# A prompt's attention between the key units of a sampling kernel: issued in smaller pieces over 21 units, with another order of value buffers

## The reference, cut to what matters

```python
o_dn = rms_norm(o_dn) * norm_w * jax.nn.silu(dn_z)          # delta rule's output
...
o_mb = moba_attend(mq, k_all, v_all, pos0)                  # blocks of 256 keys, best 3 and the own one
y = jnp.concatenate([o_dn, o_mb], axis=-1) @ w_out
...
logits = (jnp.einsum('bhqd,bhqrsd->bhqrs', qi, kg) * scale - slopes[:, None, None, None] * dist)
p = jax.nn.softmax(jnp.where(allowed, logits, NEG_INF).reshape(bsz, h, qc, r * MOBA_BLOCK), axis=-1)
out = jnp.einsum('bhqrs,bhqrsd->bhqd', p, vg)
```

## Time and profile before

| | |
|---|---|
| median of 3 runs | 1178.69 us (1176.52 to 1180.17) |
| the profiled execution | 1179.3 us |
| its span, first to last instruction | 1177.6 us |
| mean granted TensorE clock | 0.956 of 2.4 GHz |
| PE, DVE, ACT, POOL busy | 93%, 60%, 46%, 26% of the span |

### The profile page before, as it was taken

How to read it: one execution, slowest core, us unless ns; L and a number is a source line. 1 busy time by engine, 2 the same in 40 slices (tenths; PEclk the granted TensorE clock), 3 DMA queues, 4 the chain that set the end, 5 groups by cost and what they waited for, 6 DMA issues and landing times.

```text
span 1177.6 us, 20042 instructions
## 1 busy us (share of the span) xinstructions
PE 1091.5 (93%) x6991; PEld 984.7 (84%) x6991; DVE 704.3 (60%) x1200; ACT 543.8 (46%) x858; POOL 300.6 (26%) x285
## 2 busy tenths in 40 slices
PE   6999979877999999897999999989999799999997
PEld 5999869655666666486999999979999799999996
DVE  4843643666777777648666663365564866665344
ACT  3337511254766666435444443343333544444324
POOL 8400123310767677334000000223003400000111
PEclk9989969987999999798999999989999899999998
DMA  7334200356989897542444443434445244444321
GB/s 230 131 124 149 72 1 1 97 202 211 320 298 304 295 317 246 188 147 71 155 142 142 142 143 126 150 128 143 143 143 153 72 142 142 148 157 159 128 94 45
DMA packets 120882, 182.59 MB, mean 155 GB/s; under 512 B 6224, under 2 KB 61615, under 8 KB 120750
## 3 DMA queue, kind: packets, MB, share of 16 engines
q1 hardware_dynamic: 118402, 174.61, 44.7%
q0 software_dynamic: 2416, 7.16, 2.1%
HBM read 176.12 MB, written 5.63 MB: 154 GB/s over the span
## 4 chain that ended last, share of the span: by engine, by line
PE 80%; DVE 11%; issue 3%; ACT 3%; DMA 1%; POOL 0%; SPq 0%; DVEq 0%; ACTq 0%; POOLq 0%
PE bank L1724 74%; PE bank L2035 4%; DVE kTl L1147 2%; DVE lo L1140 1%; DMA raw<-w_in_mix 1%; DVE xres L1571 1%; ACT hi L748 1%; DVE xres L1147 1%; PE bank L2235 0%; PE bank L2166 0%; DVE sbias L1445 0%; DVE gs L1441 0%; DVE sbias L1436 0%; DVE xl L1578 0%; ACT kTh L748 0%
## 5 line engine op out<-in xcount | busy, mean ns | idle before, releaser
L1724 PE MATMUL bank<-xh,hi 128*128 128x320 f32 x1184 | 373.2, 315 | 27.1 <-DVE xl L1578 18.3
L1724 PE MATMUL bank<-xl,hi 128*128 128x320 f32 x1184 | 370.2, 313 | 0.0
L1724 PE MATMUL bank<-xh,lo 128*128 128x320 f32 x1184 | 369.7, 312 | 0.0
L1140 DVE TENSOR_TENSOR lo<-raw,hi 128x2048 fp32r<-128x2048 f32 x102 | 241.4, 2366 | 188.5 <-ACT hi L748 188.5
L748 ACT ACTIVATE hi<-raw 128x2048 fp32r (+2 forms) x112 | 205.3, 1833 | 113.6 <-PE bank L1724 110.7
L1724 PEld LDWEIGHTS bank<-xh,hi 128*128 128x128 f32 x1184 | 226.3, 191 | 31.1 <-issue 25.8
L1724 PEld LDWEIGHTS bank<-xl,hi 128*128 128x128 f32 x1184 | 226.6, 191 | 0.1
L1724 PEld LDWEIGHTS bank<-xh,lo 128*128 128x128 f32 x1184 | 226.2, 191 | 0.0
L1724 PE MATMUL bank<-hh,hi 128*128 128x320 f32 x416 | 129.5, 311 | 1.3 <-DVE hraw L1147 1.3
L1724 PE MATMUL bank<-hh,lo 128*128 128x320 f32 x416 | 128.6, 309 | 0.0
L1724 PE MATMUL bank<-hl,hi 128*128 128x320 f32 x416 | 128.5, 309 | 0.0
(11 more groups left out here) (397 smaller groups left out, 1554.6 us busy)
## 6 DMA issues: line engine op xcount, KB each, us to landing
raw<-w_up SPq DMA_DIRECT2D x44, 1024.0 KB
kring<-cache_k SPq DMA_DIRECT2D x88, 256.0 KB, 3.7
vring<-cache_v SPq DMA_DIRECT2D x88, 256.0 KB, 4.8
raw<-w_down SPq DMA_DIRECT2D x8, 2048.0 KB
raw<-w_in_mix SPq DMA_DIRECT2D x6, 2048.0 KB
raw<-cache_k SPq DMA_DIRECT2D x40, 256.0 KB, 3.6
raw<-cache_v SPq DMA_DIRECT2D x40, 256.0 KB, 5.1
raw<-w_in_sc SPq DMA_DIRECT2D x8, 1024.0 KB
```

The lines of the kernel that those rows point to most:

```text
L1140: dve.tensor_tensor(lo[:, p], weight(n)[:, :, 256 * p:256 * p + 256], hi[:, p], ALU.subtract)\
L1724: return pe.matmul(out, lhsT, rhs, start=start, stop=stop, **kw)
```

## The change

The prompt's work is laid over units 0 to 20 instead of 0 to 15; the last five are units 0 to 4 of round 1. Exponential, normalisation, gate product and halves of the delta rule's output are done in two pieces of two heads each (two instructions where there was one). The maxima, exponentials and divisions of the two query tiles stand at separate units, as do the copies of V's rows. TensorE's stages move from units 0, 1, 4, 6, 11, 13 to 0, 2, 7, 10, 15, 19, and the third group of the turn becomes a stage of its own at 17. That group goes into bank 5, after ACT has copied the first group from it (new wait on pTsb0), no longer into bank 7. `own_scores(0)` waits for kvtok5, since it uses bank 7. `pT` moves by 512 columns, to the ring's last two value pairs. The value pages' order becomes: the two pairs in `raw` first, then the ring's four. SP's wait for po1 moves from key group 6 to group 8, and a wait for pT2 comes in at group 7. The output weights' second half waits for all but two value pairs, before for all but four. The table of exponentials on ACT is loaded at unit 1 instead of 0. The numbers of the key units' own steps do not change.

```diff
-        pT = vr[:, 1536:3072]
-        PROMPT = {0: "sums", 1: "kv0", 4: "scores", 6: "kv1", 11: "turn", 13: "values"}
+        pT = vr[:, 2048:3584]
+        PROMPT = {0: "sums", 2: "kv0", 7: "scores", 10: "kv1", 15: "turn", 17: "turn1", 19: "values"}
...
-        vpages = [vring[:, i] for i in range(4)] + [spare_raw[:, 4:6], spare_raw[:, 6:8]]
+        vpages = [spare_raw[:, 4:6], spare_raw[:, 6:8]] + [vring[:, i] for i in range(4)]
...
-                if n == V_LAG // 2:
+                if n == V_LAG // 2 + 1:
+                    PE.wait(sp_, "pT2")
+                if n == V_LAG // 2 + 2:
                     PE.wait(sp_, "po1")
...
-            sp_.wait_ge(s["v_lo"], VALL - 4)
+            sp_.wait_ge(s["v_lo"], VALL - 2)
...
             def prompt(u):
-                if u == 0:
-                    o_logs((2, 3))
+                if u in (0, 1):
+                    o_logs((2 + u,))
+                if u == 1:
                     act.preload_act_table(ACT.Exp)
+                if u in (2, 3):
+                    x = slice(2 * u - 4, 2 * u - 2)
                     AC.wait(act, "oln3")
-                    AC.up(act.activation(qg[:, :, :], qg[:, :, :], ACT.Exp, scale=-0.5), "orn")
-                if u == 3:
-                    DV.wait(act, "mixo")
-                    AC.up(copy(xh[:, 0:4, :], oT), "mixh_done")
+                    AC.up(act.activation(qg[:, x, :], qg[:, x, :], ACT.Exp, scale=-0.5), f"orn{u - 2}")
+                if u == 5:
                     act.wait_ge(s["stores"], 16 * 7)
-                    kv_rows(range(3))
-                if u == 7:
-                    kv_rows(range(3, 6))
-                if u in (8, 9):
-                    for h in range(H):
-                        t, i = u - 8, 4 * (u - 8) + h
+                    DV.wait(act, "on11")
+                    kv_rows((0, 1))
+                if u in (6, 7):
+                    x = slice(2 * u - 12, 2 * u - 10)
+                    DV.wait(act, f"mixo{u - 6}")
+                    AC.up(copy(xh[:, x, :], oT[:, x, :]), f"mixh{u - 6}")
+                if u == 6:
+                    kv_rows((2,))
+                if 9 <= u <= 12:
+                    for i in (2 * u - 18, 2 * u - 17):
+                        t, h = divmod(i, H)
                         DV.wait(act, f"pmax{t}")
                         x = pl0[:, h, :] if t == 0 else pl1[:, h, :]
                         AC.up(act.activation(x, x, ACT.Exp, bias=pst[:, 0, i:i + 1], accum_out=pst[:, 1, i:i + 1]),
                               f"pexp{i}")
-                if u == 12:
-                    for g in range(3):
+                if 11 <= u <= 13:
+                    kv_rows((u - 8,))
+                if u in (16, 18):
+                    for g in ((0, 1) if u == 16 else (2,)):
                         PE.wait(act, f"pT{g}")
-                        AC.up(copy(pT[:, 512 * g:512 * g + 512], bank[5 + g][:, :]), f"pTsb{g}")
-                if u == 15:
+                        AC.up(copy(pT[:, 512 * g:512 * g + 512], bank[(5, 6, 5)[g]][:, :]), f"pTsb{g}")
+                if u == 20:
                     for t in range(2):
...
-                    if b == 0:
-                        prompt(u)
+                    prompt(b * UNITS + u)
...
-                if u == 1:
-                    AC.wait(dve, "orn")
-                    DV.up(tt(oT, oT, qg[:, :, :], ALU.mult), "on1")
-                if u == 2:
-                    DV.wait(dve, "on1")
-                    DV.up(dve.scalar_tensor_tensor(out=oT, in0=oT, scalar=vec(0, PA_NW), in1=zsb[:, :, :], op0=ALU.mult,
-                                                   op1=ALU.mult), "mixo")
-                if u == 4:
-                    AC.wait(dve, "mixh_done")
-                    DV.up(tt(xl[:, 0:4, :], oT, xh[:, 0:4, :], ALU.subtract), "mixl_done")
-                if u == 5:
+                if u in (3, 4):
+                    x = slice(2 * u - 6, 2 * u - 4)
+                    AC.wait(dve, f"orn{u - 3}")
+                    DV.up(tt(oT[:, x, :], oT[:, x, :], qg[:, x, :], ALU.mult), f"on1{u - 3}")
+                if u in (5, 6):
+                    x = slice(2 * u - 10, 2 * u - 8)
+                    DV.wait(dve, f"on1{u - 5}")
+                    DV.up(dve.scalar_tensor_tensor(out=oT[:, x, :], in0=oT[:, x, :], scalar=vec(0, PA_NW), in1=zsb[:, x, :],
+                                                   op0=ALU.mult, op1=ALU.mult), f"mixo{u - 5}")
+                if u in (7, 8):
+                    x = slice(2 * u - 14, 2 * u - 12)
+                    AC.wait(dve, f"mixh{u - 7}")
+                    DV.up(tt(xl[:, x, :], oT[:, x, :], xh[:, x, :], ALU.subtract), f"mixl{u - 7}")
+                if u == 8:
...
-                if u == 6:
+                if u == 9:
...
-                if u in (5, 6):
-                    t, x = u - 5, (pl0, pl1)[u - 5]
+                if u in (8, 10):
+                    t, x = (u - 8) // 2, (pl0, pl1)[(u - 8) // 2]
...
-                if u in (10, 11):
-                    t, x = u - 10, (pl0, pl1)[u - 10]
+                if u in (11, 13):
+                    t, x = (u - 11) // 2, (pl0, pl1)[(u - 11) // 2]
...
-                if u == 15:
+                if u == 20:
...
-                if stage == "turn":
+                if stage in ("turn", "turn1"):
                     AC.wait(pe, "kvtok5")
                     for g, (x, c0, t) in enumerate(((pl0, 0, 0), (pl1, 0, 1), (pl1, P, 1))):
+                        if (g < 2) != (stage == "turn"):
+                            continue
                         DV.wait(pe, f"pnorm{t}")
+                        if g == 2:
+                            AC.wait(pe, "pTsb0")
                         for h in range(H):
-                            ins = pe.transpose(bank[5 + g][:, P * h:P * h + P], x[:, h, c0:c0 + P], ident[:, :])
+                            ins = pe.transpose(bank[(5, 6, 5)[g]][:, P * h:P * h + P], x[:, h, c0:c0 + P], ident[:, :])
                         PE.up(ins, f"pT{g}")
...
-                    if b == 0 and u in PROMPT:
-                        prompt(PROMPT[u])
+                    if n in PROMPT:
+                        prompt(PROMPT[n])
...
+                        if b == 0:
+                            AC.wait(pe, "kvtok5")
```

## The result

The changed kernel took 1166.97 us (median of four runs, 1164.68 to 1173.07) against 1178.84 us before (four runs, 1176.52 to 1180.17): a ratio of 0.991 with an interval of 0.9895 to 0.9927, that is 8.6 to 12.4 us less. In a second set of five runs it was 1166.23 us and 0.990 (0.9881 to 0.9919). The forecast was 1171.2 us, 7.5 us less, with a range of 1167.5 to 1178.0.

A forecast was written before the change was run, and what follows sets the result against it. TensorE bounds the kernel, with 14.6 us idle plus low clock before turn(0). The walk's 10.5 us, less 2.5 clock and 0.5 hand-offs, gave 7.5; 1179.3 - 7.5 - 0.6 = 1171.2 us, range 1167.5 to 1178.0.

The forecast's parts named there:

- The walk: New lists stepped from the first key transpose (235.94): turn(0), the first probabilities' turn, at 285.3, 10.5 us earlier.
- One sign was missed: Sign named for the forecast: TensorE idle time before turn(0) below 8 us.
- Two were passed: Signs named for the forecast: turn(0) near 288 and the value stage near 278.
- The table load: ACT's table load, one unit later: 1.28 us, with the skill's 1.38 us drain left out.
- The middle: Prompt's scores to its turn: 13.0 us of DVE work in 15.1 us; new kvtok5 and pTsb0 waits taken as nothing.
- The loads: First value pages go to the spare weight-buffer half without a wait; sync queue's new waits cost nothing, up to 1 us.
- A condition, and nothing by itself: New value-page places gain nothing alone; with the old wait, pages landing near 285 would hold ACT nearly 10 us.
- The other end: Late in the phase: output weights' second half issued some 4.4 us later relative to its surroundings, hidden by 6 us.
- The clock, -2.5 us, and the hand-offs, -0.5: Deductions from the walk's 10.5 us: low-clock stretches 2.5 us (bounds 0 and 6), hand-offs some 0.5 us.
- The rival that the clock eats the gain: Thinly spread prompt work leaves 256 to 285 mostly at 1.2 GHz; gain 2 to 5 us, about 1175.2; chance 0.19.
- The rival that the pace does not change: Hand-offs keep prompt units at 2.81 us over 21 units; turn(0) at 298.8, 3 us late, 1181.7; chance 0.12.
- The rival that loads give the gain back: Turn(0) comes early but later rounds wait for their pages, or late output weights cost it; about 1178.7; chance 0.09.

The follow-up runs named there:

- after: The changed kernel in its first set of four runs, median 1166.97 us; its profiled run is the slowest, 1173.07 us.
- after_again: The changed kernel measured and profiled a second time with no edit: 1166.23 us, ratio 0.9900 to the kernel before.
- order_alone: The kernel before with only the new places and waits of the value pages: 1177.93 us, ratio 1.0005.
- pieces_alone: The changed kernel with the old order of value buffers, SP's old po1 wait and no new pT2 wait: 1174.45 us, ratio 0.9969 to before.
- whole_steps: The changed kernel with exponential, normalisation, gate product and output halves again over four heads in one step: 1170.68 us, ratio 0.9941 to before.
- whole_filled: whole_steps with sixteen unread matmuls on TensorE ahead of its wait before the prompt's scores: 1165.31 us, ratio 0.9905 to before.
- before: The kernel without the change: 1178.84 us, median of four runs.

## Why the prediction was right, and which term was wrong

**The bound.** Idle and low clock in the stretch ahead of turn(0) were what could be won. Behind the history's transposes the span is the same within 0.4 us, and the full round is 27.67 us again; what else moved, between turn(0) and turn(1) and in the third segment, is the clock.

**The walk.** Each point of it, with what `after` shows: unit 3's score 242.5 (243.21); the prompt's scores 250.9 (251.36); its turn 270.25 (270.11); third group of the turn 273.0, no wait (272.90, no wait); values 276.3 (276.56); first value split 275.7 (275.46, no wait); round 0's chain on DVE 273.1 to 281.7 (first step 273.02, last low half of it 281.60); turn(0) 285.3 (285.70). The walk starts at 235.94 and `after` at 235.59, so each measured step is 0.35 us later than these pairs show. From start to turn(0) the walk had 49.4 us, and the runs have 50.11 and 49.34. A list walked with durations from the earlier trace rows was right to a us over 50, in part because its errors cancel. Unit 3's score came 1.06 us later from the start than in the walk (0.71 in `after_again`); that goes with a low clock in the first four us, 0.50 and 0.58 from 236 to 240, where TensorE has no wait. The scores and the values, 3.25 us each in the walk, took 2.89 and 2.84: the 3.25 was the row of the old values and no length at full clock. The splitting was counted as four DVE and three ACT steps, and the page has three and two more. One sign was missed: TensorE idles 9.4 us before turn(0), not below 8. Two were passed: turn(0) was said near 288 and the values near 278, with the clock's cost in them.

**The table load** costs its own 1.28 us and nothing behind it. ACT's timeline in `after`:

```profile
242.77 1.28 ACT L918 ACT_TABLE_LOAD   x1
244.07 0.60 ACT L751 ACTIVATE kTh<-bank 128x512 fp32r<-128x512 f32 x1
```

It starts when the instruction before it ends (242.23 + 0.53), and the next copy starts 0.02 us after its end. Leaving out the 1.38 us that the Trainium skill gives on top ("ScalarE: Activation LUTs", section "What ACT_TABLE_LOAD costs") was right; the trace doesn't agree with that part.

**The middle.** DVE's list from the scores to the turn needed about the 15 us that it was given (15.9 us from the end of the scores, 254.25, to the turn; the walk had 16.1). The new waits for kvtok5 and pTsb0 cost nothing, as said.

**The loads.** "A condition, and nothing by itself" was shown from both sides: order_alone 0, pieces_alone 8 us short, 4.5 of them by the stall. The walk put the stall at "nearly 10 us"; ACT waited 7.52, and turn(0) came 4.5 us late. The other end: the output weights were issued at 490.17 (said: 491) and first split without a wait at 504.71, against 494.11 and 511.39. No page or weight was waited for in the profile of `after`.

**The clock, -2.5 us, and the hand-offs, -0.5: this is the term that failed.** It was charged ahead of turn(0), and there the runs have 49.34 and 50.11 us against the walk's 49.4 without it: at most 0.8 us for both, or some 1.5 if the walk's too long scores and values are set against it. The lower level came, in the first four us and at 260 to 264 (0.60), but the second of these lies under DVE's full list, so slower matmuls only filled idle time (whole_steps against whole_filled shows it); and at 252 to 256, where `before` had 0.57, `after` has 1.00: the scores ran 2.89 us instead of 4.55. A price turned up where the sum had none: behind turn(0), 2.6 us in one execution of the changed kernel and none in the other (1.5, 1.5 and 2.3 in three of its variants). The miss is 3 to 4 us: the gain was 10.5 to 11.8 us, and the sum had 10.5 by the lists before the 3.0 us of this term came off. The lower bound of the clock's part, 0, would have given 1168.7. What the timed runs paid behind turn(0) on average no profile shows.

**The rival that the clock eats the gain** had the sign of the effect wrong. It took from the earlier trace rows that spreading work thin brings the clock down. The spread cut idle pieces as well, and the mean clock to turn(0) rose from about 0.84 (0.86 and 0.77) to 0.91 and 0.93. The Trainium skill ("TensorE: Matmul & The Clock Gate", section "HAM oscillation — how this bites in real kernels") advises, for matmuls on few rows, to do all tiles of a block in one go before the next wait for a DMA, so that TensorE stays warm. The runs agree with it that an idle piece costs the clock (whole_steps against whole_filled, 4.2 to 5.4 us). No run here has the prompt's work in one block; what they show is that the wider spread, with less idle time, kept more of the clock than the narrower one.

**The rival that the pace does not change** is excluded: the twenty units ahead of the values (235.59 to 276.56) took 2.05 us each and not 2.81. **The rival that loads give the gain back** is excluded by the round of 27.67 us without a DMA wait.

## What to carry to other kernels

Where two engines work through one strict list for a third, spread a side job over more units, and cut its steps where a long one leaves the third engine idle: the halves alone and the order alone gave nothing here, spread and order together 7 us (whole_steps), all three 11 us, and unread matmuls in place of the halves as much (whole_filled). The spread with neither halves nor order was not run. Before moving work earlier, look for the first load that is issued behind it, since that one decides whether the gain arrives. Charge a low clock to the matmuls that another engine's list waits for, as the scores here, and to full stretches of TensorE; under another engine's full list it cost nothing.

## What the runs showed of the hardware

TensorE's granted clock fell from 2.4 GHz to means of 0.5 to 0.6, near its 1.2 GHz level, behind idle pieces of 1.36 us (284.81 in `after`) to 2.25 us (whole_steps, ahead of its scores), and not each time: behind 1.39 us ahead of the scores it stayed at 1.00 in both executions of the changed kernel, and the same program with the same list went at 0.59 and 0.56 from 284 to 292 in one execution and at 1.00 in another, for 2.6 us. The spread of this kernel's times goes with it (1164.7 to 1173.1 in the first set, mean clock 0.956 in the slowest run, 0.963 to 0.968 in the other three), and a single profile of it can be 6 us off its median. Unread matmuls in a wait of 2.25 us gained 5.4 us by the medians and 4.2 by the ratios; as many ahead of turn(0), where the profile has the clock at 1.00, gained nothing in the time. The stretch ahead of the first key transpose, untouched by any edit, took 233.98 to 237.03 us.
